# One expert step of a mixture-of-experts kernel: each 64-column tile makes every second SwiGLU column, and one full transpose replaces two half ones

## The chip, the cores and the metric

The kernel runs on one core of one Trainium2 chip. The metric is the device time of one execution in microseconds (us). The profiled execution is a separate one, taken with the hardware profiler; its rows are what the trace shows.

## What is computed

One inference step of a small trunk with one layer: token mixing, then a mixture of experts over 640 tokens with 1024 features. The change lies in the experts. Each token goes to 8 of 64 SwiGLU experts; an expert has a hidden width of 256. Cut from the reference:

```
def step(acc, blk):
    toks, gates, e = blk
    xb = x_pad[toks]
    hb = jax.nn.silu(xb @ p['w_e_gate'][e]) * (xb @ p['w_e_up'][e])
    yb = (hb @ p['w_e_down'][e]) * gates[:, None].astype(xb.dtype)
    return acc.at[toks].add(yb), None
```

`w_e_gate[e]` and `w_e_up[e]` are 1024 x 256, `w_e_down[e]` is 256 x 1024, all in float32.

## The kernel before

Everything but the bookkeeping is float32. The program has four stages: projection, attention and scan (to about 440 us of the profiled execution), routing and the shared expert (`route`), the expert loop (`experts`, from about 575 to 1326 us) and `combine`, which adds the parts of each token and normalises. The change touches `experts` alone.

The loop handles blocks of `SB` = 64 token slots of one expert; `U` = 4 blocks are a round, and 116 blocks run. The order of work is written out by hand for each engine and held together by counting semaphores. Per block:

- SyncE (`load_gu`, `load_down`, L1701 to L1719) loads the expert's gate and up weights (1 MB each) into one of four ring buffers and the down weights (1 MB) into another, up to four blocks ahead, and skips the load when the buffer already holds that expert. A ring buffer holds, for each partition, 8 x 256 columns of gate and then 8 x 256 of up.
- GpSimd gathers the 64 tokens as two halves of 512 features on 128 partitions (L1819) and, at the end, scatters the result (L1832).
- TensorE: `ids` (L1933) finds which tokens a block has; `turn` (L1943) transposes the gathered tokens with four full 128 x 128 transposes; `gate_up` (L1956) multiplies them by the weights; `body` transposes the hidden tile (L1967) and makes the down products (L1980).
- ScalarE copies the turned tokens to SBUF (L1846), takes SiLU (L1855) and scales the result (L1860). VectorE multiplies SiLU by up (L1914), copies the transposed hidden tile to SBUF (L1916) and prepares the next blocks' slots (L1873 to L1891).

Only 64 tokens are in a block, so a matmul fills 64 of the array's 128 columns. `gate_up` runs two such tiles beside each other: for each of 8 feature slices `kk`, the tile `h` = 0 multiplies the 64 tokens by 256 gate columns into partitions 0 to 63 of a bank, and the tile `h` = 1 by 256 up columns into partitions 64 to 127. Both read their weights contiguously. So the gate stands on the lower partitions and up on the upper; SiLU reads the lower ones and writes the upper ones (`up_lane`), the product is made there, and the hidden tile is 64 partitions x 256. It is turned by two transposes of 64 partitions x 128 columns, the even hidden columns and then the odd ones (`kk:F:2`), because the down weights are laid out so that partition p holds the rows 2p and 2p + 1.

The order on TensorE in `body` of block i is: `gate_up` of block i + 1, the transposes of block i's hidden tile, `turn` of block i + 2, `ids` of block i + 5, the down products of block i. So the SiLU and the product of block i run beside the gate/up products of block i + 1, and the copy of the transposed tile (L1916) beside `turn` and `ids`.

Other places that the rows below name: the shared expert transposes its hidden tile with a stride of two (L1651, `hid[t % 2][:, kk:F:2]`); L686 has 64 columns of `pt[c % 2][:, kk:512:KD]`, a stride of eight, as the stationary operand of an ordinary matmul; L717 transposes 32 x 128 tiles with a stride of 16; L1248 transposes contiguous 81 x 128 tiles.

Of the kernel before, what the change touches and what calls it, by code (L numbers as in the profile page):

```python
# [26 lines left out]
ALU = mybir.AluOpType  # L27
ACT = mybir.ActivationFunctionType
AX = mybir.AxisListType

P = 128
D = 1024
KD = D // P
# [25 lines left out]
F = 256  # L59
# [3 lines left out]
SB = 64  # L63
MAXB = TOK // SB
MAXR = 96
RING = [0, 1, 3, 2]
# [1655 lines left out]
def experts(nc, k, a, scope, block):  # L1722

    sem, bank, ident = k.sem, k.bank, k.ident
    sb = k.scoped(scope)
    hot = [sb(f"hot{i}", [P, NT, SB], BF16) for i in range(2)]
# [6 lines left out]
    spare = k.hT[:, :, :].rearrange("p k n -> p (k n)")  # L1736
    xT = [spare[:, i * 512:(i + 1) * 512] for i in range(2)]
    yo = [spare[:, (2 + i) * 512:(3 + i) * 512] for i in range(U)]
    sgate = [spare[:, 3072 + i * F:3072 + (i + 1) * F] for i in range(2)]
    hid = [spare[:, 3584 + i * F:3584 + (i + 1) * F] for i in range(2)]  # L1740
    hidT = [spare[:, 4096 + i * P:4096 + (i + 1) * P].rearrange("p (k n) -> p k n", k=2) for i in range(2)]
    up_lane = slice(SB, P)

    hot_ready, ids_ready, found_ready, toks_ready, late_ready = (
        sem(n) for n in ("hot_ready", "ids_ready", "found_ready", "toks_ready", "late_ready"))
# [96 lines left out]
    @block.scalar  # L1842
    def _(act):
        def turned(it, u):
            act.wait_ge(xg_t, it * U + u + 1)
            act.activation(xT[u % 2], bank[2][:, :], ACT.Copy).then_inc(xT_ready, 1)  # L1846
        act.wait_ge(k.shared_out, 2 * NT)
        turned(0, 0)
        turned(0, 1)
        act.wait_ge(k.table_ready, 1)  # L1850

        def body(it, u, final=False):
            i, par = it * U + u, u % 2
            act.wait_ge(gu_ready, i + 1)
            act.activation(sgate[par][up_lane, :], bank[par][0:SB, 0:F], ACT.Silu).then_inc(silu_ready, 1)  # L1855
            if not (final and u + 2 >= U):
                turned(*ahead(it, u, 2))
            act.wait_ge(late_ready, i + 1)
            act.wait_ge(dn_ready, i + 1)
            act.activation(yo[u], bank[4 + par][:, :], ACT.Copy, scale=gain[u][:, :]).then_inc(yo_ready, 1)  # L1860
        every_round(act, body)

    @block.vector
    def _(dve):
        def onehot(it, u):
            i, par = it * U + u, u % 2
            e, b = look(dve, 0, it, u, NE - 1), look(dve, 1, it, u, SB * MAXB)
            if not (first(it) and u < 2):
                dve.wait_ge(ids_ready, i - 1)
            shape = [P, NT, SB]  # L1870
            slot = k.slots[:, bass.ds(b, SB)].unsqueeze(1).to_broadcast(shape)
            place = k.place[:, bass.ds(e, 1), :].rearrange("p o t -> p (o t)").unsqueeze(2).to_broadcast(shape)
            dve.tensor_copy(info[par][:, :, 5:9], k.wparts[:, :, bass.ds(e, 1), :].rearrange("p t o n -> p t (o n)"))  # L1873
            dve.tensor_tensor(hot[par][:, :, :], slot, place, ALU.is_equal).then_inc(hot_ready, 1)  # L1874

        def tokens(it, u):
            i, par = it * U + u, u % 2
            dve.wait_ge(ids_ready, i + 1)
            f = found[par]
            dve.tensor_reduce(f[:, :], bank[6][:, 0:9].rearrange("p (x n) -> p x n", n=3), axis=AX.X, op=ALU.add).then_inc(found_ready, 1)  # L1880
            dve.wait_ge(found_ready, i + 1)
            dve.tensor_scalar(toks[u][:, :], f[:, 0:1], k.half[:, :], None, ALU.add)
            dve.tensor_copy(kept[u][:, :], f[:, 1:3]).then_inc(toks_ready, 1)  # L1883

        def late(it, u):
            i = it * U + u
            dve.wait_ge(toks_ready, i + 1)
            if not first(it):
                dve.wait_ge(added[u], it * 16)
            dve.tensor_scalar(dest[u][:, :], kept[u][:, 0:1], k.half[:, :], None, ALU.add)  # L1890
            dve.tensor_copy(gain[u][:, :], kept[u][:, 1:2]).then_inc(late_ready, 1)  # L1891

        dve.wait_ge(k.table_ready, 1)
        for par in range(2):
            dve.tensor_copy(info[par][:, :, 0:5], k.ids[:, :, :])
        onehot(0, 0)
        onehot(0, 1)
        k.hidden(NT - 2)
        tokens(0, 0)
        onehot(0, 2)  # L1900
        k.hidden(NT - 1)
        tokens(0, 1)
        onehot(0, 3)
        tokens(0, 2)
        onehot(1, 0)
        tokens(0, 3)
        onehot(1, 1)
        late(0, 0)
        tokens(1, 0)

        def body(it, u, final=False):
            i, par = it * U + u, u % 2
            dve.wait_ge(silu_ready, i + 1)
            dve.tensor_tensor(hid[par][up_lane, :], sgate[par][up_lane, :], bank[par][up_lane, 0:F], ALU.mult).then_inc(hid_ready, 1)  # L1914
            dve.wait_ge(hid_t, i + 1)
            dve.tensor_copy(hidT[par], bank[7][:, 0:P].rearrange("p (k n) -> p k n", k=2)).then_inc(hidT_ready, 1)  # L1916
            if not (final and u + 1 >= U):
                late(*ahead(it, u, 1))
            if not final:
                tokens(*ahead(it, u, U + 1))  # L1920
                onehot(*ahead(it, u, U + 2))
        every_round(dve, body)

    @block.tensor
    def _(pe):
        def ids(it, u):
            i, par = it * U + u, u % 2
            pe.wait_ge(hot_ready, i + 1)
            if not (first(it) and u == 0):
                pe.wait_ge(toks_ready, i)  # L1930
            for t in range(NT):
                for h in range(2):
                    last = pe.matmul(bank[6][h * SB:(h + 1) * SB, 0:9], lhsT=hot[par][:, t, :], rhs=info[par][:, t, :],  # L1933
                                     start=(t == 0), stop=(t == NT - 1))
            last.then_inc(ids_ready, 1)

        def turn(it, u):
            i = it * U + u
            pe.wait_ge(gathered[u], it * 16 + 16)
            if not (first(it) and u == 0):  # L1940
                pe.wait_ge(xT_ready, i)
            for j in range(4):
                last = pe.transpose(bank[2][:, j * P:(j + 1) * P], xg[u][:, j * P:(j + 1) * P], ident[:, :])  # L1943
            last.then_inc(xg_t, 1)

        def gate_up(it, u):
            i, par = it * U + u, u % 2
            pe.wait_ge(k.gu_in[u], it * 32 + 32)
            pe.wait_ge(xT_ready, i + 1)
            if not (first(it) and u < 2):  # L1950
                pe.wait_ge(hid_ready, i - 1)
            w = k.ring[RING[u]]
            for kk in range(KD):
                lhsT = xT[par][:, (kk % 4) * P + (kk // 4) * SB:(kk % 4) * P + (kk // 4 + 1) * SB]
                for h in range(2):
                    last = pe.matmul(bank[par][h * SB:(h + 1) * SB, 0:F], lhsT=lhsT, rhs=w[:, (h * KD + kk) * F:(h * KD + kk + 1) * F],  # L1956
                                     start=(kk == 0), stop=(kk == KD - 1))
            last.then_inc(gu_ready, 1)

        def body(it, u, final=False):  # L1960
            i, par = it * U + u, u % 2
            if not (final and u + 1 >= U):
                gate_up(*ahead(it, u, 1))
            pe.wait_ge(hid_ready, i + 1)
            pe.sem_inc(waited, 1)
            for kk in range(2):
                last = pe.transpose(bank[7][:, kk * SB:(kk + 1) * SB], hid[par][up_lane, kk:F:2], ident[up_lane, up_lane])  # L1967
            last.then_inc(hid_t, 1)
            if not (final and u + 2 >= U):
                turn(*ahead(it, u, 2))  # L1970
            if not final:
                ids(*ahead(it, u, U + 1))
            pe.wait_ge(k.dn_in[u], it * 16 + 16)
            pe.wait_ge(hidT_ready, i + 1)
            if not (first(it) and u < 2):
                pe.wait_ge(yo_ready, i - 1)
            down = k.dn[RING[u]]
            for kk in range(2):
                for h in range(2):
                    last = pe.matmul(bank[4 + par][h * SB:(h + 1) * SB, :], lhsT=hidT[par][:, kk, :],  # L1980
                                     rhs=down[:, kk * D + h * 512:kk * D + (h + 1) * 512], start=(kk == 0), stop=(kk == 1))
            last.then_inc(dn_ready, 1)
        ids(0, 0)
        k.rest(NT - 2)
        ids(0, 1)
        k.rest(NT - 1)
        turn(0, 0)
        ids(0, 2)
        gate_up(0, 0)
        turn(0, 1)  # L1990
        ids(0, 3)
        ids(1, 0)
        pe.wait_ge(k.table_ready, 1)
        every_round(pe, body)


# [224 lines left out]
```

## Time and profile before

| | |
|---|---|
| median of 3 runs | 1416.13 us (1404.22 to 1416.46) |
| the profiled execution's time | 1407.8 us |
| its span, first to last instruction | 1406.0 us |
| mean granted TensorE clock over the span | 0.955 |
| TensorE matmuls busy | 1298.2 us, 92% of the span |
| TensorE weight loads (beside the matmuls) | 738.9 us, 53% |
| VectorE / ScalarE / GpSimd busy | 566.6 / 339.1 / 320.8 us |

PE stands for TensorE's matmuls and PEld for its weight loads (the stationary operand), DVE for VectorE, ACT for ScalarE, POOL for GpSimd, SPq for SyncE's issuing of transfers. A float32 matmul leaves two weight loads and two matmul records. A record's end is modelled, so where rates are wanted, the distance of starts is read. The granted clock is a share of 2.4 GHz.

### The profile page before, as it was taken

To read this page: it belongs to the slowest core of one execution; us is meant where nothing else is said; L and a number is where in the kernel's file an instruction comes from. 1 tells how busy PE (TensorE), PEld (TensorE's weight loads), DVE (VectorE), ACT (ScalarE), POOL (GpSimd) and SP (SyncE) were. 2 spreads that over 40 slices of the span, in tenths; PEclk is the share of its full clock that TensorE was granted. 3 is DMA by queue.
4 is the path that set the end of the run, shared out by engine and by line. 5 is a ranking of instruction groups with operands and counts; after the bars stand their busy time and mean duration, and the time that the engine had idled before them with its cause. 6 is when DMAs were issued, how large, how long until landed. Compare 5 with 4: busy or idle time off the path is not lost. (4 is left out here: it accounts for less than half of the span.)

```text
span 1406.0 us, 27016 instructions
## 1 busy us (share of the span) xinstructions
PE 1298.2 (92%) x8994; PEld 738.9 (53%) x8994; DVE 566.6 (40%) x1726; ACT 339.1 (24%) x675; POOL 320.8 (23%) x390
## 2 busy tenths in 40 slices
PE   4998999978989869899999999999999999999766
PEld 3543644856754434555555555555555555555322
DVE  1272367377814344233333333333333333333168
ACT  4121011165122211222222222222222222222111
POOL 4021140040010000233232333333332323233101
PEclk9799799989999969999999999999999999999878
DMA  9856533471254330744696798989998998673195
GB/s 355 254 149 194 187 124 127 158 211 69 88 215 172 130 140 1 303 168 153 264 400 239 287 406 324 417 317 419 364 418 339 412 404 351 253 285 126 54 431 226
DMA packets 90153, 349.10 MB, mean 248 GB/s; under 512 B 22661, under 2 KB 27924, under 8 KB 62592
## 3 DMA queue, kind: packets, MB, share of 16 engines
q1 hardware_dynamic: 68208, 300.31, 55.7%
q0 software_dynamic: 21040, 46.67, 9.1%
q10 hardware_dynamic: 864, 1.57, 0.3%
q8 instruction: 25, 0.41, 0.1%
q14 instruction: 16, 0.13, 0.0%
HBM read 484.32 MB, written 46.87 MB: 378 GB/s over the span
## 5 line engine op out<-in xcount | busy, mean ns | idle before, releaser
L1956 PE MATMUL banks<-rings,hT 128*64 128x256 f32 x3712 | 420.0, 379 | 1.9 <-ACT hT L1846 1.2
L1956 PEld LDWEIGHTS banks<-rings,hT 128*64 128x64 f32 x3712 | 261.4, 137 | 189.4 <-issue 67.9
L1980 PE MATMUL banks<-downs,hT 128*64 128x512 f32 x928 | 223.2, 602 | 0.9 <-issue 0.9
L1819 POOL DMA_INDIRECT h<-h2D,toks x117 | 118.2, 1010 | 455.3 <-DVE kept L1883 435.0
L1846 ACT ACTIVATE hT<-banks 128x512 f32<-128x512 f32 x116 | 69.3, 597 | 378.0 <-PE banks L1943 377.9
L1832 POOL DMA_INDIRECT yD<-hT,dest x116 | 118.1, 1018 | 132.7 <-ACT hT L1860 130.2
L1916 DVE COPY hT<-banks 128x128 f32<-128x128 f32 x116 | 33.8, 292 | 255.1 <-PE banks L1967 255.1
L1860 ACT ACTIVATE hT<-banks,gain 128x512 f32<-128x512 f32 x116 | 79.7, 687 | 180.5 <-PE banks L1980 180.5
L1980 PEld LDWEIGHTS banks<-downs,hT 128*64 128x64 f32 x928 | 56.2, 138 | 68.7 <-issue 68.7
L1873 DVE COPY info<-wparts 128x20 bf16 x118 | 21.2, 180 | 153.8 <-issue 152.7
L1943 PE MATMUL banks<-ident,h 128*128 128x128 f32 x464 | 76.1, 287 | 0.0
L1914 DVE TENSOR_TENSOR hT<-hT,banks 64x256 f32<-64x256 f32 x116 | 49.2, 424 | 66.2 <-ACT hT L1855 65.8
L1605 PE MATMUL banks<-rings,mixedT 128*128 128x512 f32 x160 | 71.1, 604 | 3.7 <-PEq L2137 3.7
L767 PE MATMUL banks<-hT,rings 128*128 128x512 f32 (+1 forms) x256 | 73.7, 447 | 0.0
L767 PEld LDWEIGHTS banks<-hT,rings 128*128 128x128 f32 x256 | 40.2, 195 | 38.8 <-issue 37.9
L1967 PEld LDWEIGHTS banks<-ident,hT 64*128 64x128 f32 x232 | 35.9, 202 | 46.9 <-issue 46.9
L1874 DVE TENSOR_TENSOR hot<-slots,place 128x320 bf16 x118 | 58.1, 493 | 0.0
L1967 PE MATMUL banks<-ident,hT 64*128 64x64 f32 x232 | 51.7, 303 | 1.8 <-DVE hT L1914 1.8
L1943 PEld LDWEIGHTS banks<-ident,h 128*128 128x128 f32 x464 | 48.7, 140 | 8.6 <-issue 0.9
L1605 PEld LDWEIGHTS banks<-rings,mixedT 128*128 128x128 f32 x160 | 30.7, 194 | 41.3 <-issue 41.3
L677 PE MATMUL banks<-rings,cS 128*32 128x512 f32 x192 | 30.4, 713 | 23.3 <-DMA rings<-w_ada 23.3
L342 POOL TENSOR_TENSOR modrow<-modrow,brow 2x512 f32<-2x512 f32 x8 | 12.1, 1511 | 148.4 <-ACT modrow L401 148.4
(453 smaller groups left out, 1477.7 us busy)
## 6 DMA issues: line engine op xcount, KB each, us to landing
rings<-w_e_gate SPq DMA_DIRECT2D x116, 1024.0 KB
rings<-w_e_up SPq DMA_DIRECT2D x116, 1024.0 KB
downs<-w_e_down SPq DMA_DIRECT2D x116, 1024.0 KB
rings<-w_ada SPq DMA_DIRECT2D x12, 2048.0 KB, 11.3
rings<-yD SPq DMA_DIRECT2D x8, 2048.0 KB, 17.3
rings<-w_in SPq DMA_DIRECT2D x4, 2048.0 KB, 12.4
rings<-matD SPq DMA_DIRECT2D x3, 2048.0 KB, 14.3
matD<-rings SPq DMA_DIRECT2D x2, 2048.0 KB
```

Source lines behind the costliest of these rows:

```text
L767: last = pe.matmul(out[:, 0:n], lhsT=w[:, kk, j * P:(j + 1) * P], rhs=hT[:, kk, lo:lo + n], start=(kk == 0), stop=(kk == KD - 1))
L1605: last = pe.matmul(bank[2 * (t % 2) + h][:, :], lhsT=k.mixedT[:, kk, t * P:(t + 1) * P], rhs=wout[h][:, kk, :], start=(kk == 0), stop=(kk ...
L1819: pool.indirect_dma_start(out=xg[u], out_offset=None, in_=k.h2D, bounds_check=2 * TOK - 1, oob_is_err=False, in_offset=bass.IndirectOffset ...
L1832: pool.indirect_dma_start(out=k.yD, out_offset=bass.IndirectOffsetOnAxis(ap=dest[u][:, 0:1], axis=0), in_=yo[u], in_offset=None, bounds_ch ...
L1846: act.activation(xT[u % 2], bank[2][:, :], ACT.Copy).then_inc(xT_ready, 1)
L1860: act.activation(yo[u], bank[4 + par][:, :], ACT.Copy, scale=gain[u][:, :]).then_inc(yo_ready, 1)
L1874: dve.tensor_tensor(hot[par][:, :, :], slot, place, ALU.is_equal).then_inc(hot_ready, 1)
L1914: dve.tensor_tensor(hid[par][up_lane, :], sgate[par][up_lane, :], bank[par][up_lane, 0:F], ALU.mult).then_inc(hid_ready, 1)
L1943: last = pe.transpose(bank[2][:, j * P:(j + 1) * P], xg[u][:, j * P:(j + 1) * P], ident[:, :])
L1956: last = pe.matmul(bank[par][h * SB:(h + 1) * SB, 0:F], lhsT=lhsT, rhs=w[:, (h * KD + kk) * F:(h * KD + kk + 1) * F], start=(kk == 0), sto ...
L1967: last = pe.transpose(bank[7][:, kk * SB:(kk + 1) * SB], hid[par][up_lane, kk:F:2], ident[up_lane, up_lane])
L1980: last = pe.matmul(bank[4 + par][h * SB:(h + 1) * SB, :], lhsT=hidT[par][:, kk, :], rhs=down[:, kk * D + h * 512:kk * D + (h + 1) * 512], ...
```

## The change

Each of the two tiles now makes gate and up columns: the tile `h` takes the gate columns h, h + 2, h + 4 ... (128 of them) and the same up columns, as one moving operand of 2 x 128 columns that is read from the ring buffer with a stride of two. Partition h x 64 + n of the bank then holds, for token n, 128 gate columns and 128 up columns. SiLU and the product work on 128 partitions x 128 columns, and the hidden tile is 128 x 128. One full transpose turns it, and its output columns are already the even and the odd half that the down products expect. The loads, the down products and everything else are as before.

```
-    sgate = [spare[:, 3072 + i * F:3072 + (i + 1) * F] for i in range(2)]
-    hid = [spare[:, 3584 + i * F:3584 + (i + 1) * F] for i in range(2)]
+    FH = F // 2
+    sgate = [spare[:, 3072 + i * FH:3072 + (i + 1) * FH] for i in range(2)]
+    hid = [spare[:, 3584 + i * FH:3584 + (i + 1) * FH] for i in range(2)]
...
-    up_lane = slice(SB, P)
...
-            act.activation(sgate[par][up_lane, :], bank[par][0:SB, 0:F], ACT.Silu).then_inc(silu_ready, 1)
+            act.activation(sgate[par], bank[par][:, 0:FH], ACT.Silu).then_inc(silu_ready, 1)
...
-            dve.tensor_tensor(hid[par][up_lane, :], sgate[par][up_lane, :], bank[par][up_lane, 0:F], ALU.mult).then_inc(hid_ready, 1)
+            dve.tensor_tensor(hid[par], sgate[par], bank[par][:, FH:F], ALU.mult).then_inc(hid_ready, 1)
...
-            w = k.ring[RING[u]]
+            w = k.ring[RING[u]].rearrange("p (x k f) -> p k x f", x=2, k=KD)
             for kk in range(KD):
                 lhsT = xT[par][:, (kk % 4) * P + (kk // 4) * SB:(kk % 4) * P + (kk // 4 + 1) * SB]
                 for h in range(2):
-                    last = pe.matmul(bank[par][h * SB:(h + 1) * SB, 0:F], lhsT=lhsT, rhs=w[:, (h * KD + kk) * F:(h * KD + kk + 1) * F],
+                    last = pe.matmul(bank[par][h * SB:(h + 1) * SB, 0:F].rearrange("p (x f) -> p x f", x=2), lhsT=lhsT,
+                                     rhs=w[:, kk, :, h:F:2],
                                      start=(kk == 0), stop=(kk == KD - 1))
...
-            for kk in range(2):
-                last = pe.transpose(bank[7][:, kk * SB:(kk + 1) * SB], hid[par][up_lane, kk:F:2], ident[up_lane, up_lane])
-            last.then_inc(hid_t, 1)
+            pe.transpose(bank[7][:, 0:P], hid[par], ident[:, :]).then_inc(hid_t, 1)
```

All lines from L1725 on move down by one, and by two fewer from the down products on. On TensorE's queue one block of the loop stands as follows before (`rings` are the weight buffers, `hT` the memory that holds the tokens and the hidden tiles, `h_1` the gathered tokens, `info` and `hot` the slots; the size is that of the output):

```order
L1956 MATMUL banks<-rings,hT 64x256 x16
L1967 MATMUL banks<-ident,hT 128x64 x2
L1943 MATMUL banks<-ident,h_1 128x128 x4
L1933 MATMUL banks<-info,hot 64x9 x10
L1980 MATMUL banks<-downs,hT 64x512 x4
```

And in the changed kernel, at the same place of the queue:

```order
L1957 MATMUL banks<-rings,hT 64x256 x16
L1968 MATMUL banks<-ident,hT 128x128
L1944 MATMUL banks<-ident,h_1 128x128 x4
L1934 MATMUL banks<-info,hot 64x9 x10
L1980 MATMUL banks<-downs,hT 64x512 x4
```

Two transposes have become one of the size of the four behind it; the sixteen gate/up matmuls keep their number, size and place, and nothing has changed places. The order on the other engines is the same instruction by instruction; SiLU and the product have other shapes.

## Rows read from the trace of the kernel before

**Rows 1.** The page's costliest group: line, engine, shapes, records; busy us, mean ns; idle.
```profile
L1956 PE MATMUL banks<-rings,hT 128*64 128x256 f32 x3712 | 420.0, 379 | 1.9 <-ACT hT L1846 1.2
```

**Rows 2.** Busy us per stage: PE, PEld, DVE, ACT, POOL; clock, DMA share, GB/s.
```profile
900.00:1100.00 200.00, 200.00 (x1739) 112.12 (x1739) 64.93 (x279) 51.43 (x93) 62.86 (x62) 1.00 0.93 377
```

**Rows 3.** Timeline of PE (start, length, records): second block, one mid-loop, a late one.
```profile
587.26 3.62 PE L1956 MATMUL banks<-rings,hT 128*64 128x256 f32 x32
...
902.82 3.62 PE L1956 MATMUL banks<-rings,hT 128*64 128x256 f32 x32
906.37 0.45 PE L1967 MATMUL banks<-ident,hT 64*128 64x64 f32 x2
906.74 0.66 PE L1943 MATMUL banks<-ident,h 128*128 128x128 f32 x4
907.33 0.32 PE L1933 MATMUL banks<-info,hot 128*64 128x9 bf16 x10
907.51 1.91 PE L1980 MATMUL banks<-downs,hT 128*64 128x512 f32 x8
909.26 3.62 PE L1956 MATMUL banks<-rings,hT 128*64 128x256 f32 x32
...
1302.10 3.62 PE L1956 MATMUL banks<-rings,hT 128*64 128x256 f32 x32
```

**Rows 4.** Timeline of PE: the loop's start; then one group of four transposes, cut shorter twice.
```profile
574.54 3.67 PE L1956 MATMUL banks<-rings,hT 128*64 128x256 f32 x32 [1.20 <-ACT hT L1846]
578.14 0.66 PE L1943 MATMUL banks<-ident,h 128*128 128x128 f32 x4
...
580.76 3.67 PE L1956 MATMUL banks<-rings,hT 128*64 128x256 f32 x32 [0.71 <-issue]
584.37 0.45 PE L1967 MATMUL banks<-ident,hT 64*128 64x64 f32 x2
...
900.30 0.66 PE L1943 MATMUL banks<-ident,h 128*128 128x128 f32 x4
...
900.47 0.49 PE L1943 MATMUL banks<-ident,h 128*128 128x128 f32 x3
...
900.58 0.38 PE L1943 MATMUL banks<-ident,h 128*128 128x128 f32 x2
```

**Rows 5.** Timeline of DVE and ACT beside these blocks (in brackets: idle before, releaser).
```profile
900.41 0.29 DVE L1916 COPY hT<-banks 128x128 f32<-128x128 f32 x1 [2.21 <-PE banks L1967]
...
903.81 0.38 ACT L1855 ACTIVATE hT<-banks 64x256 f32<-64x256 f32 x1
904.21 0.42 DVE L1914 TENSOR_TENSOR hT<-hT,banks 64x256 f32<-64x256 f32 x1 [0.55 <-ACT hT L1855]
```

**Rows 6.** Weight loads by line and shape (busy us, mean ns of one).
```profile
L1956 PEld LDWEIGHTS banks<-rings,hT 128*64 128x64 f32 x3712 | 261.4, 137 | 189.4 <-issue 67.9
L1943 PEld LDWEIGHTS banks<-ident,h 128*128 128x128 f32 x464 | 48.7, 140 | 8.6 <-issue 0.9
L686 PEld LDWEIGHTS banks<-sel,part 128*64 128x64 f32 x64 | 7.5, 216 | 3.3 <-issue 3.3
L1651 PEld LDWEIGHTS banks<-ident,tmp 128*128 128x128 f32 x10 | 1.7, 201 | 1.0 <-issue 0.9
```

**Rows 7.** Timeline of PEld: runs of weight loads back to back.
```profile
26.99 2.00 PEld L686 LDWEIGHTS banks<-sel,part 128*64 128x64 f32 x16 [0.84 <-issue]
...
61.36 1.84 PEld L717 LDWEIGHTS banks<-ident,qT 32*128 32x128 f32 x16
...
390.77 0.67 PEld L1248 LDWEIGHTS banks<-ident,y 81*128 81x128 f32 x8
```

**Rows 8.** Busy us per stage, as rows 2: two stretches with the loads of L686.
```profile
26.90:29.10 2.20, 2.20 (x24) 2.09 (x24) 0.00 (x0) 0.60 (x1) 0.00 (x0) 1.00 1.04 386
38.40:42.00 3.60, 3.60 (x36) 3.46 (x32) 0.00 (x0) 1.88 (x2) 0.00 (x0) 0.50 1.11 185
```

**Rows 9.** Busy us per stage, as rows 2: a stretch at a full DMA share.
```profile
1040.00:1060.00 20.00, 20.00 (x178) 11.27 (x176) 6.28 (x27) 4.98 (x9) 6.77 (x7) 1.00 1.02 420
```

## The prediction

> **What bounds the kernel now.** I first read the busy times (table above): the PE, TensorE's matmul side, is busy for 92% of the span. Of the groups the costliest is L1956, the gate/up products of the expert loop [rows 1]: 3712 records are 116 blocks x 16 matmuls x 2, since one float32 matmul leaves two records.
>
> Then the busy time by stage [rows 2]: for 200 us in the middle of the loop the PE is busy for all 200.00, at a granted clock of 1.00; VectorE is busy for 65, ScalarE for 51, and the DMA engines for a share of 0.93. So the loop is an unbroken PE stream.
>
> The PE's timeline shows one block [rows 3]. Gate/up starts at 902.82, the pair of transposes at 906.37 (3.55 later), the four transposes of a later block's tokens at 906.74 (0.37), the ten id matmuls at 907.33 (0.59), the down products at 907.51 (0.18), and the next gate/up at 909.26 (1.75). The sum is 6.44, and it doesn't change: from 587.26 to 1302.10 there are 111 such steps, 714.84 / 111 = 6.44. No row has an idle time. A microsecond added to or taken from the PE's work in a block is therefore worth 116 of them, as long as no other engine becomes later than the PE.
>
> **The change, part by part.**
>
> *Two transposes become one.* Today the pair takes 0.37 from its start to the start of the next group [rows 3]. The new one has the form of L1943: 128 partitions, 128 contiguous columns, the full identity. The next group is L1943 itself, so it is a fifth transpose in front of four of its kind. From the start of its second, three of the four spread over 0.49 us; from the start of its third, two spread over 0.38 [rows 4]. So they start 0.11 apart, which is the price, and one lasts 0.27. It should also begin where the pair began: with the pair it starts 3.61 after its gate/up (580.76 to 584.37), and in the one early block without a pair the four start 3.60 after it (574.54 to 578.14) [rows 4]. Gain: 0.37 - 0.11 = 0.26 a block, 116 x 0.26 = 30.2 us.
>
> *ScalarE and VectorE.* SiLU and the product go from 64 partitions x 256 to 128 x 128, half the columns. Today they take 0.38 and 0.42 and end at 904.63 [rows 5]; the PE wants the result at 906.37, 1.74 later. I cost the saving at nothing: the PE's next gate/up hides it in every block but the last, where at most some 0.3 us once could show.
>
> *The copy of the transposed tile* (L1916) starts 0.11 after the four transposes do (900.41 against 900.30) and lasts 0.29 [rows 4, 5]; the down products wait for it and start 0.77 after the four (906.74 to 907.51) [rows 3]. The new transpose starts 0.11 ahead of the four and lasts 0.27 [rows 4], so its result stands 0.16 after their start, and with the copy's start the same 0.03 behind and its 0.29 the tile is there after 0.48: 0.29 of cover is left. If that cover went, its excess would be paid in each block (0.1 us is 11.6 us).
>
> *Gate/up with a stride of two.* There are as many matmuls as before, each over as many columns (256, now 128 of gate and 128 of up); the loaded tokens and the accumulation stay. What is new is that the moving operand's columns lie 8 bytes apart. No matmul of the trace streams such an operand, so I bound the price from both sides.
>
> Lower bound: nothing. The matmul takes the columns as fast as now, 16 pairs (the two 64-column tiles run together) in 3.55, or 0.222 a pair. I exclude a gain: nothing becomes shorter.
>
> Upper bound: the nearest rows are the weight loads, the PE's other read of SBUF. Contiguous, 128 columns for a transpose load in 140 ns (L1943); with a stride of two in 201 (L1651) [rows 6]. For ordinary float32 matmuls, 64 contiguous columns take 137 (L1956), and with a stride of eight 216 (L686). As a rate, back to back: sixteen strided loads of 128 columns (L717) take (1.84 - 0.20) / 15 = 0.109 us each (less the last one's length), or 0.85 ns a column, against at most (0.67 - 0.14) / 7 = 0.076 contiguous (L1248) [rows 7]. The ordinary load L686 needs (2.00 - 0.22) / 15 = 0.119 for half as many columns, so it seems to read each column twice, once for each half of the float32 product that a record makes. This is the read and not the array: at a granted clock of 1.00 L686 loads 16 in 2.00 us, and at 0.50 it loads 32 in 3.46 [rows 7, 8].
>
> Now the moving stream: 0.222 us for 256 columns is 0.87 ns a column. If a record reads each column twice, as the load does, a read takes 0.43 ns today and would take 0.85 strided: 512 x 0.85 = 0.435 a pair, 0.213 more, x 16 = 3.41 a block, x 116 = 395.6 us. The difference of the single loads L1651 and L1943 (61 ns for 128, 0.48 ns a read) would give 0.244 a pair and 453 us, but it holds a fixed part that a rate does not.
>
> If a record reads each column once and holds it for both halves, it needs one read in 0.87 ns, the strided read just keeps up, and the price is the lower bound. That is what decides. I take the upper bound by rate: the load has the same two halves and demonstrably pays for both, and its next load runs under the current stream, so the halves look like separate passes.
>
> *A rule against this.* The Trainium skill's page "SBUF — State Buffer", section "SBUF: two separate sides", says that reads are slowed by crossing into a new 16-byte line, so that four float32 elements is as far as one strides for free. By it a stride of two is free, and the sum would be 1377.6. The trace disagrees for weight loads, where a stride of two already costs (201 against 140) [rows 6]; for a moving operand no row here speaks.
>
> **Sum**, against the profiled execution's own 1407.8 us (span 1406.0): 1407.8 - 30.2 + 395.6 = 1773.2; the block becomes 6.44 - 0.26 + 3.41 = 9.59. The median of the three runs, 1416.13, lies 8.3 above that execution, so a median after may too; I say 1775.
>
> **Rivals.**
>
> *The stride is free* (the other side). 1407.8 - 30.2 = 1377.6. For it: 0.87 ns a column is as slow as the strided read, so it decides itself at one read a column. Against it: the double price of L686. The Trainium skill's rule above would have it so. Here the DMA would be next: 6.18 for 6.44 asks 4% more of 377 GB/s [rows 2], 393, while stretches at a full share move 420 [rows 9]. The loads run up to four blocks ahead, so a few microseconds of waits at most: 1376 to 1385. Chance 0.27, of which 0.02 for a gain that waits eat to under 1%.
>
> *Only one of the two reads pays*: 198 instead of 396, so 1576. Nothing in the rows has such a half price. Chance 0.04.
>
> *The two tiles' strided streams share one read path*: a pair would take four times 0.213 instead of twice, another 6.8 a block, 2566. Against it: the pairs run together today in 3.55 for 16. Chance 0.03.
>
> *The clock falls*, since the array is fed every other cycle. The level below 1.00 that the rows show is 0.50 (1.2 of 2.4 GHz) [rows 8]; the rest of the block, 2.63, would double and the strided stream would not: 1773 + 116 x 2.63 = 2078. Against it: the PE never goes idle in the loop, and the granted clock stayed at 1.00 through the strided loads at 27 to 29 us [rows 8]. Chance 0.03.
>
> **How the numbers follow.** The doubled read has 0.63 and its own range 1755 to 1800 (a little hidden work below, part of the single-load price above). Beside it stand 0.27 for free, 0.04, 0.03 and 0.03. Since the doubled read alone is under 8 in 10, the range must reach to the free case: 1374 to 1800. About 1% is what a measurement of this kernel can tell from no change. Slower by more: 0.63 + 0.04 + 0.03 + 0.03 = 0.73; faster by more: 0.25; within: 0.02.
>
> **What would show it.** The gate/up rows (379 ns each today) near 590 (213 more); from gate/up to the transpose 6.96 instead of 3.55; blocks 9.59 apart; the transpose 0.11 before the four; its load at 140, as L1943's; the PE still without idle time at a clock of 1.00; the DMA's share in the middle of the loop at some 0.6. I am wrong if the gate/up still spans 3.55 (the free case), if down products wait for the copy (idle time before L1980), or if the clock reads 0.50.

## The result, and the profile after

The changed kernel takes 1404.12 us (median of 20 runs, 1397.39 to 1407.65), the kernel before 1413.61 (20 runs, 1402.76 to 1416.46). The ratio is 0.9944, with a 95% interval of 0.9924 to 0.9964: faster by 0.56%, which is within 1%. The forecast was 1775 us, slower by a quarter; that 1404.12 lies inside its range of 1374 to 1800 says little, since the range was stretched across two cases and the time fell into neither.

The costliest group of the page (line, engine, shapes, records; busy us, mean ns; idle), and then the busy time in the middle of the loop (columns as in [rows 2]), both of the changed kernel:

```profile
L1957 PE MATMUL banks<-rings,hT 128*64 128x256 f32 x3712 | 440.0, 388 | 1.9 <-ACT hT L1847 1.2
```

```profile
900.00:1100.00 200.00, 200.00 (x1734) 108.24 (x1731) 58.07 (x281) 45.14 (x94) 64.06 (x63) 1.00 0.95 383
```

The gate/up records last 388 ns on average instead of 379 [rows 1], not 590. The PE is busy for all 200 us at a granted clock of 1.00 as before [rows 2], and the DMA share rose from 0.93 to 0.95. So the stream on the PE is still unbroken, and what a block costs is the sum of its pieces. Its timeline in the changed kernel (start, length, records):

```profile
594.02 3.79 PE L1957 MATMUL banks<-rings,hT 128*64 128x256 f32 x32
...
897.02 0.32 PE L1934 MATMUL banks<-info,hot 128*64 128x9 bf16 x10
897.22 1.94 PE L1980 MATMUL banks<-downs,hT 128*64 128x512 f32 x8
898.98 3.80 PE L1957 MATMUL banks<-rings,hT 128*64 128x256 f32 x32
902.72 0.33 PE L1968 MATMUL banks<-ident,hT 128*128 128x128 f32 x1
902.88 0.60 PE L1944 MATMUL banks<-ident,h 128*128 128x128 f32 x4
903.41 0.32 PE L1934 MATMUL banks<-info,hot 128*64 128x9 bf16 x10
903.59 1.91 PE L1980 MATMUL banks<-downs,hT 128*64 128x512 f32 x8
905.34 3.79 PE L1957 MATMUL banks<-rings,hT 128*64 128x256 f32 x32
909.05 0.33 PE L1968 MATMUL banks<-ident,hT 128*128 128x128 f32 x1
...
1299.27 3.79 PE L1957 MATMUL banks<-rings,hT 128*64 128x256 f32 x32
```

Read against [rows 3], from start to start:

| piece of a block | before, us | after, us |
|---|---|---|
| gate/up, to the transposes | 3.55 | 3.72 (905.34 to 909.05 reads 3.71, 898.98 to 902.72 3.74) |
| hidden tile's transposes, to the four of the tokens | 0.37 | 0.16 |
| the four, to the ids | 0.59 | 0.53 |
| ids, to the down products | 0.18 | 0.18 (now and then 0.20, as at 897.02) |
| down products, to the next gate/up | 1.75 | 1.75 (1.76 at 897.22) |
| block, mean of 111 | 6.44 | (1299.27 - 594.02) / 111 = 6.354 |

The block is 0.086 shorter, 111 x 0.086 = 9.5 us, and the medians differ by 9.5 too (by the interval of the ratio, 5 to 11). The two profiled executions differ by less (1407.8 and 1404.86), because the loop begins later in the second: gate/up of its second block starts at 587.63 for 580.76 [rows 4]. Most of that arises in a stretch that the change does not touch. First the kernel before, then the changed one, busy time from 300 to 420 us:

```profile
300.00:420.00 120.00, 108.01 (x864) 80.33 (x864) 73.98 (x147) 43.38 (x104) 15.73 (x56) 0.97 0.35 110
```

```profile
300.00:420.00 120.00, 108.20 (x855) 82.52 (x854) 75.23 (x151) 45.02 (x109) 16.55 (x56) 0.90 0.29 88
```

The mean granted clock there is 0.90 for 0.97, over time spent at the two levels (1.2 and 2.4 GHz), and fewer instructions are done (855 for 864). That the clock alone makes the delay is not shown. This is why single executions are read by their blocks below, and not by their totals alone.

### The profile page after: what moved, and what is told of

It is laid out like the page before. It is cut to its first block and busy times, and to the rows that moved or that the text cites. A ratio compares the mean times of both kernels' runs of the same rounds, so it can differ in the third digit from the quotient of the medians.

```text
span 1403.1 us, 26784 instructions
## 1 busy us (share of the span) xinstructions
PE 1297.6 (92%) x8878; PEld 724.8 (52%) x8878; DVE 538.4 (38%) x1726; ACT 315.4 (22%) x675; POOL 321.3 (23%) x390
## 5 line engine op out<-in xcount | busy, mean ns | idle before, releaser
L1957 PE MATMUL banks<-rings,hT 128*64 128x256 f32 x3712 | 440.0, 388 | 1.9 <-ACT hT L1847 1.2
L1980 PE MATMUL banks<-downs,hT 128*64 128x512 f32 x928 | 224.3, 605 | 1.1 <-issue 0.7
L1980 PEld LDWEIGHTS banks<-downs,hT 128*64 128x64 f32 x928 | 56.9, 138 | 68.9 <-issue 68.9
L1944 PE MATMUL banks<-ident,h 128*128 128x128 f32 x464 | 69.7, 273 | 0.0
L1944 PEld LDWEIGHTS banks<-ident,h 128*128 128x128 f32 x464 | 54.6, 142 | 0.9 <-issue 0.9
L1915 DVE TENSOR_TENSOR hT<-hT,banks 128x128 f32<-128x128 f32 x116 | 33.4, 288 | 40.1 <-ACT hT L1856 39.3
L1968 PEld LDWEIGHTS banks<-ident,hT 128*128 128x128 f32 x116 | 16.1, 139 | 48.8 <-issue 48.8
L885 POOL TENSOR_TENSOR bias<-skew,maskA 128x256 f32<-128x256 f32 x24 | 19.6, 855 | 87.6 <-POOLq L2137 68.3
```

Of the source, the lines that this page charges most:

```text
L1915: dve.tensor_tensor(hid[par], sgate[par], bank[par][:, FH:F], ALU.mult).then_inc(hid_ready, 1)
L1957: last = pe.matmul(bank[par][h * SB:(h + 1) * SB, 0:F].rearrange("p (x f) -> p x f", x=2), lhsT=lhsT, rhs=w[:, kk, :, h:F:2], start=(kk == ...
```

## The experiments

Of contiguous halves there are six runs, of every other kernel below a single one. Code is cut to the operands that change, and "..." in a timeline marks rows left out.

**Theories.** A: the forecast's, a strided column is read twice and each read pays (gate/up about 6.96 a block). B: a strided read costs nothing, and something else takes 0.17 us a block (the two runs of 128 columns, or both tiles reading alternate columns of one place). C: the read has a rate of its own, counted in lines of 16 bytes, and a matmul takes the longer of the array's time and the read's; at a stride of two the read is just the longer.

**Contiguous halves.** The changed kernel, but each tile takes one half of the columns in a piece; the down weights are then loaded so that a partition holds rows p and p + 128.

```
-        rhs=w[:, kk, :, h:F:2],
+        rhs=w[:, kk, :, h * FH:(h + 1) * FH],
-        sp.dma_start(dst, w[e].rearrange("(p k) n -> p (k n)", k=2))
+        sp.dma_start(dst.rearrange("p (k n) -> p k n", k=2), w[e].rearrange("(k p) n -> p k n", k=2))
```

> As the changed kernel, but the two tiles take halves (columns 0 to 127 and 128 to 255 of gate and of up, contiguous) and the down weights are loaded so that partition p holds the rows p and p + 128 (pieces of 4 KB for 8 KB). Everything is computed. If the stride costs the 0.17 us that gate/up now takes longer (3.55 to 3.72 us), gate/up falls back to 3.55, a block to 6.17, and the time to some 1404 - 116 x 0.17 = 1384 us. If the cost comes from a moving operand in two runs of 128 columns that lie 8 KB apart, gate/up stays at 3.72 and the time at 1404. If the DMA becomes late with the shorter pieces and blocks, idle time stands before gate/up or down products.

It takes 1379.18 us (median of 6, 1378.92 to 1384.49), the kernel before beside it 1412.44; the ratio is 0.9779 (0.975 to 0.9807). It beats both kernels: the lowest of the changed kernel's 20 runs is 1397.39. Its PE timeline:

```profile
903.79 3.62 PE L1957 MATMUL banks<-rings,hT 128*64 128x256 f32 x32
907.34 0.33 PE L1968 MATMUL banks<-ident,hT 128*128 128x128 f32 x1
907.50 0.60 PE L1944 MATMUL banks<-ident,h 128*128 128x128 f32 x4
908.03 0.32 PE L1934 MATMUL banks<-info,hot 128*64 128x9 bf16 x10
908.21 1.91 PE L1980 MATMUL banks<-downs,hT 128*64 128x512 f32 x8
909.96 2.33 PE L1957 MATMUL banks<-rings,hT 128*64 128x256 f32 x20
```

Gate/up is back at 3.55 (903.79 to 907.34), with the same two runs of 128 columns and the same single transpose, and the block is 6.17 (6.19 in the mean of 111, a wait for weights included). So the 0.17 belongs to the stride and the rest of the change is worth 0.27 a block. Of the 25 us between the medians of the changed kernel and this one, the blocks show 18 (0.16 each in the mean); where the rest comes from is open, and with it the 5 us by which the time is below the 1384 expected. Its busy time in mid-loop, and of its waits on the PE the one for weights in the loop (us in total, times, longest):

```profile
900.00:1100.00 200.00, 199.12 (x1772) 111.55 (x1768) 59.73 (x288) 46.48 (x96) 65.58 (x65) 1.00 0.98 394
```

```profile
PE banks L1957 <- DMA rings<-w_e_up: 0.9, 1, 0.9
```

The transfers now run at 394 GB/s and a share of 0.98, and held the PE up once, for 0.9 us. The next bound looks close.

**The stride alone.** The kernel before, with gate still in one tile and up in the other, each reading its even columns and then its odd ones; the hidden tile then comes out sorted and its two transposes read contiguously.

```
-        rhs=w[:, (h * KD + kk) * F:(h * KD + kk + 1) * F],
+        rhs=w[:, (h * KD + kk) * F:(h * KD + kk + 1) * F].rearrange("p (f x) -> p x f", x=2),
-        hid[par][up_lane, kk:F:2]
+        hid[par][up_lane, kk * P:(kk + 1) * P]
```

> The kernel before, with the stride alone: one tile makes gate, the other up, as before, but each reads its 256 columns as the 128 even and then the 128 odd ones, with a stride of two. The hidden tile then is contiguous in its two transposes. Everything is computed. If the stride or its two runs cost, gate/up takes 3.72 instead of 3.55 us here too. If the cost comes from two tiles that read alternate columns of the same place at the same time, it stays at 3.55.

PE timeline:

```profile
900.49 3.79 PE L1956 MATMUL banks<-rings,hT 128*64 128x256 f32 x32
904.21 0.33 PE L1967 MATMUL banks<-ident,hT 64*128 64x64 f32 x2
904.48 0.66 PE L1943 MATMUL banks<-ident,h 128*128 128x128 f32 x4
...
906.99 3.79 PE L1956 MATMUL banks<-rings,hT 128*64 128x256 f32 x32
```

Gate/up is 3.72 again, though the tiles now read different places: sharing a place costs nothing. The pair of transposes falls from 0.37 to 0.27 because it no longer reads with a stride. The block is 6.50 (6.44 + 0.17 - 0.10 = 6.51), the time 1415.93 us.

**The size of the stride.** The kernel before, one run of 256 columns per matmul at a stride S of 2, 3, 4 and 8 elements (8, 12, 16 and 32 bytes), from anywhere within the same tile's weights. For 2, 4 and 8:

```
-        rhs=w[:, (h * KD + kk) * F:(h * KD + kk + 1) * F],
+        rhs=w[:, h*KD*F + kk//S*S*F + kk%S : h*KD*F + (kk//S+1)*S*F : S],
```

> The kernel before, with each gate/up matmul reading 256 columns in one run with a stride of two over the weights of two feature slices; the products are those of other weights than the reference's, the work is the same. If the price belongs to the stride, gate/up takes 3.72 us as in the changed kernel. If it belongs to the jump between two runs, 3.55.

> As the run with a stride of four, with three (12 bytes; three lines for four columns) over three feature slices; the products are those of other weights. If the time goes by lines, 256 columns take 192 of the 256 lines that strides of four and more take: some three quarters of 0.460, 0.345 a pair, gate/up 5.6 us. If there is a step behind four, 3.72. If only pairs that share a line are fast and any other column is slow, something between 0.34 and 0.46 a pair.

> The kernel before, each gate/up matmul reading 256 columns in one run with a stride of four (16 bytes) over the weights of four feature slices; the products are those of other weights than the reference's. With a stride of two a pair of records took 0.227 us, with eight 0.460. If what counts is how many 16-byte lines a column costs (a half at two, a whole one from four on), four costs what eight does: gate/up 7.46 us, block 10.35. If up to four float32 elements are free and the step comes behind that, gate/up stays at 3.72.

> As the run with one stride-of-two run, with a stride of eight columns (32 bytes) over the weights of all eight feature slices; the products are those of other weights than the reference's. If the moving operand is read once a column at a rate that any stride can have, gate/up takes the same as with a stride of two (3.55 to 3.72 us). If reads are slowed once no two of them share 16 bytes, gate/up about doubles, to some 7.0 us, and the time goes to some 1800 us.

PE timelines, gate/up and the transposes behind it: S of 2, 3, 4 and 8.

```profile
901.73 3.79 PE L1956 MATMUL banks<-rings,hT 128*64 128x256 f32 x32
905.45 0.45 PE L1967 MATMUL banks<-ident,hT 64*128 64x64 f32 x2
```

```profile
904.90 5.62 PE L1956 MATMUL banks<-rings,hT 128*64 128x256 f32 x32
910.45 0.45 PE L1967 MATMUL banks<-ident,hT 64*128 64x64 f32 x2
```

```profile
902.02 7.39 PE L1956 MATMUL banks<-rings,hT 128*64 128x256 f32 x32
909.34 0.44 PE L1967 MATMUL banks<-ident,hT 64*128 64x64 f32 x2
```

```profile
905.67 7.53 PE L1956 MATMUL banks<-rings,hT 128*64 128x256 f32 x32
913.13 0.44 PE L1967 MATMUL banks<-ident,hT 64*128 64x64 f32 x2
```

| stride, elements | 16-byte lines in 256 columns | gate/up, us a block | time, us |
|---|---|---|---|
| 1 [rows 3] | 64 | 3.55 | 1413.61 (median of 20) |
| 2 | 128 | 3.72 | 1437.4 |
| 3 | 192 | 5.55 | 1648.52 |
| 4 | 256 | 7.32 | 1855.01 |
| 8 | 256 | 7.46 | 1870.85 |

One run of 256 costs the same 0.17 as two of 128, so B's first form falls. From 128 lines on, the time grows evenly: (5.55 - 3.72) / (16 x 64) = 1.79 ns a line, (7.32 - 5.55) / (16 x 64) = 1.73, and from 4 to 8 elements, where the lines are as many, only 0.14 us more. By that rate 64 lines need 16 x 64 x 1.76 = 1.80 us, half of the contiguous 3.55: there something else sets the time, by C the array. A's price is nearly there from four elements on, and not at two.

**Lines or distances.** Two variants of the kernel before take pairs of neighbouring columns, one pair every 32 bytes. In one the pairs lie inside a 16-byte line (128 lines), in the other they straddle two (256 lines); neighbours and jumps are the same. `off` is `kk % 4 * 2` in the first and 3 in the second.

```
+        rhs=w[:, (h * 2 + kk // 4) * 4 * F:(h * 2 + kk // 4 + 1) * 4 * F]
+            .rearrange("p (g e) -> p g e", e=8)[:, :, off:off + 2],
```

> The kernel before, each gate/up matmul reading 128 pairs of neighbouring columns, the pairs eight columns (32 bytes) apart and each inside one 16-byte line; the products are those of other weights than the reference's. If a pair of records costs 0.885 ns for each of its lines, twice (0.227 us for 128 lines with a stride of two, 0.340 for 192 with three, 0.452 for 256 with four), 128 lines give 0.227 us, gate/up 3.72. If the distance from one column to the next decides, jumps of 28 bytes in every second step should cost: 128 x 1.77 ns more or less on top, 0.33 to 0.34.

> The same pairs, eight columns apart, shifted so that each pair lies across the border of two lines (columns 3 and 4 of every eight); the products are those of other weights. Neighbours and jumps are those of the run before; only the lines differ: 256 for 128. If lines are what costs, 0.452 us a pair of records, gate/up 7.3, the time about 1855 us. If neighbourhood is what counts, the same as the run before.

PE timelines, inside a line and then across:

```profile
903.63 3.85 PE L1956 MATMUL banks<-rings,hT 128*64 128x256 f32 x32
907.41 0.45 PE L1967 MATMUL banks<-ident,hT 64*128 64x64 f32 x2
```

```profile
906.49 7.39 PE L1956 MATMUL banks<-rings,hT 128*64 128x256 f32 x32
913.80 0.45 PE L1967 MATMUL banks<-ident,hT 64*128 64x64 f32 x2
```

3.78 against 7.31 us (1435.48 and 1849.67 us in all): moving the same pattern by one or three columns nearly doubles the time. What counts is how many 16-byte lines are entered, which is C. Lines are not quite all: 3.78 is 0.06 more than the 3.72 of a stride of two, which enters as many, and that is open.

**Longer matmuls, and a single stream.** The kernel before; the down products read 512 columns with a stride of two, and the shared expert's gate/up (L1642, a full tile of 128 columns, so one stream alone) as well. The shared expert's transposes (L1651) then read contiguously.

```
-        rhs=down[:, kk * D + h * 512:kk * D + (h + 1) * 512]
+        rhs=down[:, kk * D + h:(kk + 1) * D:2]
-        rhs=gu[:, kk]
+        rhs=gu[:, kk].rearrange("p x (f s) -> p x s f", s=2)
-        hid[t % 2][:, kk:F:2]
+        hid[t % 2][:, kk * P:(kk + 1) * P]
```

> The kernel before with the stride of two put elsewhere, gate/up left alone: the down products read 512 columns in one run with a stride of two (the output columns come in another order than the reference's), and the shared expert's gate/up matmuls (128 columns of the array, 512 moving columns, one stream at a time) read evens and then odds, its hidden tile being contiguous when turned. If the 11 ns that a pair of 256 columns pays are a start-up cost of a matmul, a pair of down records goes from 0.427 to 0.438; if it is a price by column, to some 0.449. In the shared expert the same: if the price needs two streams beside each other, its matmuls stay as they are.

Groups by line and shape (busy us, mean ns), of the kernel before and then of this one:

```profile
L1980 PE MATMUL banks<-downs,hT 128*64 128x512 f32 x928 | 223.2, 602 | 0.9 <-issue 0.9
L1642 PE MATMUL banks<-rings,hT 128*128 128x512 f32 x80 | 37.6, 628 | 0.0
```

```profile
L1980 PE MATMUL banks<-downs,hT 128*64 128x512 f32 x928 | 231.8, 620 | 0.9 <-issue 0.9
L1642 PE MATMUL banks<-rings,hT 128*128 128x512 f32 x80 | 39.2, 646 | 0.0
L1651 PEld LDWEIGHTS banks<-ident,tmp 128*128 128x128 f32 x10 | 1.2, 140 | 1.2 <-issue 1.1
```

One group of 128 tokens in the shared expert's gate/up, on the PE's timeline before and then in this kernel:

```profile
543.78 7.13 PE L1642 MATMUL banks<-rings,hT 128*128 128x512 f32 x16
```

```profile
546.64 7.47 PE L1642 MATMUL banks<-rings,hT 128*128 128x512 f32 x16
```

By the mean lengths, whose ends are modelled, a record of 512 columns is 18 ns longer, in two tiles beside each other and in one stream alone; a record of 256 was 9 longer. By the starts it is 20 or 21: four pairs of down records take 1.83 us for 1.75 [rows 3], sixteen records of the single stream 0.34 more. The price goes by the column, not by the matmul, and needs no second stream. A record alone in the array takes about as long (7.13 / 16 = 0.45) as a pair beside each other (1.75 / 4 = 0.44), and pays the same for the stride. And L1651's load takes 140 ns once contiguous, for 201 [rows 6]: the stride had been its whole excess.

**An ordinary load with a stride of two.** The kernel before; the stationary tokens of gate/up are every second column.

```
-        lhsT = xT[par][:, (kk % 4) * P + (kk // 4) * SB:(kk % 4) * P + (kk // 4 + 1) * SB]
+        lhsT = xT[par][:, (kk % 4) * P + kk // 4:(kk % 4 + 1) * P:2]
```

> The kernel before, moving operands contiguous, but the 64 tokens that gate/up loads as the stationary operand are read with a stride of two (the tokens are mixed up, the work is the same). If a weight load pays for a stride of two where a moving stream does not, the load of gate/up goes from 137 to some 190 ns while the pairs stay at 0.216 us, since the load runs under the stream. If the load stays at 137, the rows L1651 and L1943 differ by something else than the stride.

The loads of that line (busy us, mean ns):

```profile
L1956 PEld LDWEIGHTS banks<-rings,hT 128*64 128x64 f32 x3712 | 263.9, 138 | 187.0 <-issue 67.8
```

138 ns for 137 [rows 6], gate/up stays at 379 ns a record, and the time is 1413.91 us. This ordinary load of 64 columns does not pay for a stride of two. L1651's does, and the run above showed that its stride is the reason; it is a transpose's load and has 128 columns, and which of the two matters was not tried. Nor do 16-byte lines explain it: the transposing loads of L717, with a stride of sixteen over 32 partitions, pay no more than L1651's 201 at a stride of two (kernel before):

```profile
L717 PEld LDWEIGHTS banks<-ident,qT 32*128 32x128 f32 x16 | 1.8, 199 | 0.0
```

## Why the prediction was wrong

**The failed step is the upper bound of the strided read, and taking it.** The forecast went by the rate of strided loads [rows 7], 0.85 ns a column, and by L686 seeming to read each column twice. Those loads have strides of eight and sixteen elements, where every column lies on a line of its own. At a stride of eight the moving operand does pay about what the step said: (7.46 - 3.55) / 16 = 0.244 a pair of records for the 0.213 that was forecast. But the step put that price on a stride of two, where two columns share a line and half as many are entered; there it is 0.011 a pair. The one row at a stride of two, L1651's 201 ns, seemed to bear it out, and it is a transposing load, which an ordinary load does not resemble (138 ns).

**What stands in its place.** A pair of records, one of each tile, takes the longer of the array's time and the read's, and the read takes about 1.76 ns a line. In the traces the pairs start 0.227 us apart at 128 lines, 0.340 at 192 and 0.451 at 256, each time 1.76 or 1.77 ns a line. Contiguous they start 0.216 apart, where 64 lines would need 0.113: so something else sets it, taken here to be the array. So at a stride of two the read is 11 ns the longer: 0.17 a block, 116 x 0.17 = 19.7 us, for the 3.41 a block and 395.6 us of the sum. A record alone in the array pays as much (L1642), so 1.76 is the price of a line in each record. It is about twice the 0.85 a column of L717 [rows 7], as the prediction's two reads a record would have it with lines for columns; whether a record reads twice or once at that price, no run separates. The prediction's "that is what decides" named the right comparison, read against array, and answered it with the wrong count.

**The free rival** is the nearest case, but partly by luck: its reason, one read a column that just keeps up, would let any stride keep up, and at four elements gate/up takes 7.32. "The strided read just keeps up" was off by 5% of a pair, 0.17 a block, and that took 19.7 of its 30.2 us: the time fell in neither of the two cases that held most of the chance. Without the stride its numbers come true: contiguous halves have blocks of 6.17 for its 6.18 and 394 GB/s for its 393. That 1379.18 us meets its 1377.6 is luck in part, since its sum starts from one execution's 1407.8; by the medians side by side the gain is 1412.44 - 1379.18 = 33.3 for its 30.2.

**The transposes: right in sum.** Forecast 0.26 a block. From the pair's start to the ids it was 0.37 + 0.59 = 0.96 and is 0.16 + 0.53 = 0.69, so 0.27. The start came 0.16 before the four and not 0.11; the four then took 0.06 less. The rows had this: of four transposes the first starts 0.17 before the second (900.30 to 900.47), the later ones 0.11 apart [rows 4], and the new transpose is now the first of the row. The pair's stride was 0.10 of this gain, as the stride alone shows (0.27 for 0.37 once contiguous); the step had not split it. The new load takes 140 ns, as said:

```profile
902.71 0.14 PEld L1968 LDWEIGHTS banks<-ident,hT 128*128 128x128 f32 x1 [0.41 <-issue]
```

**ScalarE, VectorE and the copy: right.** Their rows on the timeline of the changed kernel:

```profile
899.85 0.27 ACT L1856 ACTIVATE hT<-banks 128x128 f32<-128x128 f32 x1
900.15 0.29 DVE L1915 TENSOR_TENSOR hT<-hT,banks 128x128 f32<-128x128 f32 x1
...
903.08 0.29 DVE L1917 COPY hT<-banks 128x128 f32<-128x128 f32 x1 [2.64 <-PE banks L1968]
```

SiLU and the product take 0.27 and 0.29 instead of 0.38 and 0.42 [rows 5], and end 2.28 before the PE wants the tile (900.44 to 902.72): hidden. The copy ends 0.49 after the four transposes start (903.37 to 902.88), forecast 0.48, though by parts that offset each other: the transpose started 0.05 earlier than forecast and lasted 0.33 for 0.27. The down products start at 903.59, so 0.22 of cover is left for the forecast 0.29, since the four became shorter. What stays open: some blocks are longer by a few hundredths. In one block of every four (27 of the 111) the down products start 0.02 later and last 0.01 longer (as at 897.02 and 897.22), in all 0.04; in 27 others gate/up takes 3.73 or 3.74. So the mean of 6.354 lies 0.014 above the pieces' 6.34, 1.6 us in all. Contiguous halves show the first too, the kernel before and the stride alone do not; what makes it was not tried.

**The other rivals.** The clock stayed at 1.00 in mid-loop, also at a stride of eight, where gate/up takes twice as long:

```profile
900.00:1100.00 200.00, 200.00 (x1082) 74.56 (x1079) 39.96 (x172) 31.55 (x57) 38.65 (x38) 1.00 0.57 217
```

A shared read path would have made two tiles pay more than one; L1980 and L1642 pay the same 18 ns. (That rival's 2566 is a slip for 2564: twice 395.6 on top of 1773.2.) Half a price (1576) fits no row at a stride of two.

**The rule against the forecast.** The Trainium skill's page "SBUF — State Buffer", section "SBUF: two separate sides", puts the cost of a strided read on 16-byte lines, and the runs bear that out (3.78 against 7.31 us for the same pairs inside and across a line). It also lets up to four float32 elements be strided for free; for this kernel's moving operand two already cost 5% (3.72 for 3.55), three 56% (5.55) and four 106% (7.32), and the measurement decides.

## What to carry to other kernels

Cost a strided moving operand by the 16-byte lines that it enters, and set that against the array's time for the same columns; here the two crossed just below a stride of two in float32, so the stride was nearly free per matmul and still took two thirds of the gain. A price read from a row at another stride, or from a transposing load, is not a price for this read. Where a stride only sorts columns for a later step, sort in the layout of a load instead: loading the down weights by halves gave 1379 us for 1404.

## What was not expected of the hardware

- The read of the moving operand is counted in 16-byte lines: about 1.76 ns a line in each record, in two tiles beside each other as in one stream alone.
- Alignment alone nearly doubles it: with pairs of columns 32 bytes apart gate/up costs 3.78 us a block inside a line and 7.31 across two.
- A transpose's load of 128 columns pays for a stride of two (201 ns for 140), an ordinary load of 64 columns does not (138 for 137). Why the two differ is open, as is the 0.14 us a block that a stride of eight costs over a stride of four.
